# Gate products one unit earlier per section, halves of the experts without barriers, and a paired left one-hot in a two-block transformer kernel

## What is computed

```python
def peer(h, w_query, sub_keys, expert_u, expert_v):
    ...
    gates = jax.nn.softmax(best_v, axis=-1).astype(h.dtype)
    ...
        u = jnp.take(expert_u, xc["idx"], axis=0)
        vv = jnp.take(expert_v, xc["idx"], axis=0)
        a = jax.nn.gelu(jnp.einsum("td,thkd->thk", xc["h"], u))
        return jnp.einsum("thk,thkd->td", xc["g"] * a, vv)
```

## Time and profile before

| | |
|---|---|
| median of 3 runs | 3040.22 us (3030.36 to 3046.02) |
| the profiled execution | 3042.81 us, its span 3041.2 us |
| granted clock of TensorE, mean | 0.967 |
| PE busy | 2880.7 us (95%) |
| PE weight loads busy | 2668.6 us (88%) |
| DVE busy | 2273.0 us (75%) |
| ACT busy | 1364.5 us (45%) |
| POOL busy | 176.4 us (6%) |

### The profile page before, as it was taken

The page is one execution under the profiler, slowest core; times in us unless marked ns, Lnnn a source line. Parts: engine busy times, 40 slices in busy tenths (PEclk is TensorE's granted clock), DMA queues, the critical chain, the costliest instruction groups (busy, mean ns, idle before and its releaser), DMA issues.

```text
span 3041.2 us, 61140 instructions
## 1 busy us (share of the span) xinstructions
PE 2880.7 (95%) x22296; PEld 2668.6 (88%) x22296; DVE 2273.0 (75%) x3797; ACT 1364.5 (45%) x1986; POOL 176.4 (6%) x189
## 2 busy tenths in 40 slices
PE   6998988989989999999999999999999899999998
PEld 5998976889989989989988878799999899988787
DVE  6777834367777668978889978756579888899766
ACT  3445431234444545544434445545455444344454
POOL 0102002100101000020000000000000200000000
PEclk8999986989999999999999999999999999999999
DMA  8885730038867454544445578654445444455554
GB/s 335 302 289 174 242 104 1 1 134 274 302 218 255 142 184 146 180 153 161 161 150 168 166 234 289 216 173 132 160 147 182 153 159 158 148 166 166 165 193 145
DMA packets 150590, 549.51 MB, mean 181 GB/s; under 512 B 16720, under 2 KB 16976, under 8 KB 150224
## 3 DMA queue, kind: packets, MB, share of 16 engines
q1 hardware_dynamic: 127584, 464.05, 45.4%
q0 software_dynamic: 22176, 80.75, 8.0%
q10 hardware_dynamic: 720, 3.17, 0.3%
HBM read 546.86 MB, written 1.05 MB: 180 GB/s over the span
## 4 chain that ended last, share of the span: by engine, by line
PE 69%; DVE 8%; ACT 2%; issue 1%; POOLq 0%; DMA 0%; DVEq 0%; POOL 0%; ACTq 0%
PE acc L2073 15%; PE st L1600 12%; PE st L1604 11%; PE st L1601 11%; PE acc L2079 7%; DVE w_lo L808 3%; PE st L2044 3%; PE acc L1604 1%; PE acc L1601 1%; PE acc L1600 1%; DVE arena L1271 1%; ACT w_hi L424 1%; PE acc L2004 1%; PE st L1651 1%; DVE arena L1306 1%
## 5 line engine op out<-in xcount | busy, mean ns | idle before, releaser
L808 DVE TENSOR_TENSOR w_lo<-ring,w_hi 128x1024 fp32r<-128x1024 f32 x864 | 1076.1, 1247 | 502.2 <-ACT w_hi L424 494.8
L424 ACT ACTIVATE w_hi<-ring 128x1024 fp32r<-128x1024 f32 x864 | 910.5, 1054 | 892.0 <-PE st L1604 798.0
L1600 PE MATMUL st<-h_hi,w_hi 128*128 128x256 f32 x4080 | 1016.3, 287 | 7.0 <-ACT arena L736 3.5
L1601 PE MATMUL st<-h_lo,w_hi 128*128 128x256 f32 x4080 | 1003.7, 284 | 0.0
L1600 PEld LDWEIGHTS st<-h_hi,w_hi 128*128 128x128 f32 x4080 | 783.7, 192 | 20.0 <-issue 11.2
L1601 PEld LDWEIGHTS st<-h_lo,w_hi 128*128 128x128 f32 x4080 | 784.7, 192 | 0.0
L1604 PE MATMUL st<-h_hi,w_lo 128*128 128x256 f32 x4080 | 577.8, 284 | 21.9 <-DVE w_lo L808 21.8
L1604 PEld LDWEIGHTS st<-h_hi,w_lo 128*128 128x128 f32 x4080 | 527.8, 192 | 27.9 <-DVE w_lo L808 27.7
L2073 PE MATMUL acc<-w_hi,act_hi 128*128 128x512 f32 x1016 | 322.6, 399 | 3.9 <-DVE act_lo L1391 3.9
L2073 PE MATMUL acc<-w_hi,act_lo 128*128 128x512 f32 x1016 | 316.1, 392 | 0.0
L769 ACT ACTIVATE act_hi<-arena 128x256 fp32r (+1 forms) x256 | 106.6, 418 | 409.4 <-PE acc L2079 401.1
(11 more groups left out here) (311 smaller groups left out, 2890.2 us busy)
## 6 DMA issues: line engine op xcount, KB each, us to landing
ring<-weights SPq DMA_DIRECT2D x864, 512.0 KB, 3.4
arena<-ada_weights POOLq DMA_DIRECT2D x104, 512.0 KB, 5.0
extra<-ada_weights POOLq DMA_DIRECT2D x48, 512.0 KB, 4.5
arena<-ada_weights SPq DMA_DIRECT2D x16, 512.0 KB, 13.2
arena<-const ACTq DMA_DIRECT2D x1, 2112.0 KB, 10.9
x_t<-params SPq DMA_DIRECT2D x1, 1024.0 KB, 11.3
extra<-crows POOLq DMA_DIRECT2D x2, 512.0 KB, 5.3
out<-arena SPq DMA_DIRECT2D x4, 256.0 KB, 2.2
```

Of the source, the lines that this page charges most:

```text
L424: nc_a.activation(w_hi[:, u % 2, :], ring[:, u % RING, :], ACT.Copy).then_inc(hi_ready, 1)
L808: v.tensor_tensor(w_lo[:, u % 2, :], ring[:, u % RING, :], w_hi[:, u % 2, :], ALU.subtract)\
L1600: mm(dst(t), w, hi_t(t), start=start, stop=False, skip_group_check=True)
L1601: mm(dst(t), w, lo_t(t), start=False, stop=False, skip_group_check=True)
```

## The change

The turns of a half are cut into four sections of eight turns (`SECTIONS`, `PER`). In the last turn of each section there is one unit where there were two (`alone=True`), so from one section to the next the gates come one unit sooner: those of turn 31 now come behind unit 61 and not behind unit 63. The stages `peer_b` and `peer_c` are gone on all engines. In their place ACT waits for the count of multiplies (`g_mult`) ahead of the first `upper` of each half of the rows, DVE waits for all gelus (`gelu`) once, POOL waits for the count of gate products (`g_psum`), and v unit 0 starts the accumulation itself in place of `clear_acc`. `hot_l` is laid out with two tokens innermost, compared with `pair_iota`, so that the weights of one token are read with a step of two.

```diff
+SECTIONS = 4
+PER = TURNS // SECTIONS
...
-        hot_l = [ar(512 * b, 512, base=extra).bitcast(BF16).rearrange("p (t n) -> p t n", t=GROUP) for b in range(2)]
+        hot_l = [hots(512 * b, 512) for b in range(2)]
...
-                def u_half(first, between=None):
+                def u_half(first, between=None, behind=None):
...
                         gelu_of(n)
+                        if n == first + HALF - SECTIONS + 1 and behind is not None:
+                            behind()
                         if n + 1 < first + HALF:
                             step(base + n + 1)
...
-                stage(eng, ST[f"peer_b{l}"])
...
+                def first_gated():
+                    eng.wait_ge(sem("g_mult"), 2 * TURNS * l + TURNS)
+                    upper(0)
+                    upper(1)
+
+                u_half(HALF, behind=first_gated)
...
-                        if n + 2 < first + HALF:
+                        if n + 2 < NKEYS:
                             eng.wait_ge(used, nth(v_base + n))
+                            if n + 2 == HALF:
+                                eng.wait_ge(sem("g_mult"), 2 * TURNS * (l + 1))
                             upper(n + 2)
...
-                    v.tensor_tensor(hot_l[g % 2], keys_t[:, 0, tokens(g, i)].unsqueeze(2).to_broadcast([P, GROUP, NKEYS]),
-                                    kc("iota").unsqueeze(1).to_broadcast([P, GROUP, NKEYS]), ALU.is_equal)\
+                    v.tensor_tensor(hot_l[g % 2], spread(keys_t[:, 0, :], g, i, NKEYS),
+                                    pair_iota.unsqueeze(1).to_broadcast([P, GROUP // 2, NKEYS, 2]), ALU.is_equal)\
...
+                    for part_ in range(SECTIONS):
+                        g, n = PER * part_, (2 * PER - 1) * part_
+                        if part_ == 0:
+                            turn(half, 0, 0)
+                            if half == 1:
+                                eng.wait_ge(sem("gelu"), NKEYS * (l + 1))
+                            g, n = 1, 2
+                        with eng.Fori(0, PER // 2 - 1) as i:
+                            for k in range(2):
+                                turn(half, g + k, n + 2 * k, i)
+                        if part_ > 0:
+                            turn(half, g + PER - 2, n + 2 * PER - 4)
+                        turn(half, PER * part_ + PER - 1, (2 * PER - 1) * part_ + 2 * PER - 2, alone=True)
...
-                stage(eng, ST[f"peer_b{l}"])
+                step(base + NKEYS - 4)
+                step(base + NKEYS - 3)
+                multiply(0, TURNS - 1)
                 lower(0)
                 lower(1)
+                step(base + NKEYS - 2)
+                step(base + NKEYS - 1)
                 turns(1, v_turn)
-                stage(eng, ST[f"peer_c{l}"])
                 v_base = base + NKEYS
-                lower(HALF)
-                lower(HALF + 1)
+                for n in range(HALF - 4, HALF):
+                    if n == HALF - 2:
+                        multiply(1, TURNS - 1)
+                    lower(n + 2)
+                    step(v_base + n)
...
-                for half in range(2):
-                    stage(eng, ST[("peer_b", "peer_c")[half] + str(l)])
                 if l == 0:
+                    eng.wait_ge(sem("g_psum"), 2 * TURNS)
                     eng.dma_start(c_row, crows[1]).then_inc(sem("c_back"), 16)
...
-                                     hot_l[g % 2][:, k, :], hot_r[g % 2][part_][:, k // 2, :, k % 2],
+                                     hot_l[g % 2][:, k // 2, :, k % 2], hot_r[g % 2][part_][:, k // 2, :, k % 2],
...
+                    unit(2)
+                    for part_ in range(SECTIONS):
+                        g, n = PER * part_, (2 * PER - 1) * part_ + 3
+                        with eng.Fori(0, PER // 2 - 1) as i:
+                            for k in range(2):
+                                token_gates(half, g + k, i)
+                                unit(n + 2 * k, i)
+                                unit(n + 2 * k + 1, i)
+                        token_gates(half, g + PER - 2)
+                        unit(n + 2 * PER - 4)
+                        unit(n + 2 * PER - 3)
+                        token_gates(half, g + PER - 1)
+                        unit(n + 2 * PER - 2)
                     unit(HALF - 1)
-                    token_gates(half, TURNS - 1)
...
-                                   w_hi[:, u % 2, 512 * half:512 * half + 512], start=False, stop=False,
+                                   w_hi[:, u % 2, 512 * half:512 * half + 512],
+                                   start=n == 0 and i is None and act_part is act_hi, stop=False,
                                    skip_group_check=True)
...
-                stage(eng, ST[f"peer_b{l}"])
-                clear_acc()
                 turns(1, v_unit)
-                stage(eng, ST[f"peer_c{l}"])
```

More of the change, by code:

```diff
@@ L354, in build @@
         for l in range(LAYERS):
-            for name in ("out", "peer_b", "peer_c", "peer_d"):
+            for name in ("out", "peer_d"):
                 ST[f"{name}{l}"] = len(ST) + 1
@@ L760, in _ @@
                 nc_a.activation(gate_t, st[:, 3, 0:T], ACT.Copy).then_inc(sem("selt"), 1)
-                u_half(HALF)
-                stage(eng, ST[f"peer_b{l}"])
                 def upper(n, i=None):
@@ L769, in upper @@
                     nc_a.activation(act_hi[:, n % 2, :], src, ACT.Copy).then_inc(sem("gated_hi"), 1)
+                def first_gated():
[3 more added lines that the diff above has]
+                u_half(HALF, behind=first_gated)
                 def v_half(first):
                     v_base = base + NKEYS
-                    upper(first)
-                    upper(first + 1)
                     with eng.Fori(0, HALF // 4 - 1) as i:
@@ L1393, in turns, with u_turn @@
                 def turns(half, turn):
-                    turn(half, 0)
-                    with eng.Fori(0, TURNS // 2 - 1) as i:
-                        for g in range(2):
-                            turn(half, 1 + g, i)
-                    turn(half, TURNS - 1)
-                    multiply(half, TURNS - 1)
-                def u_turn(half, g, i=None):
-                    u = base + HALF + 2 * g
+                    for part_ in range(SECTIONS):
[11 more added lines that the diff above has]
+                        turn(half, PER * part_ + PER - 1, (2 * PER - 1) * part_ + 2 * PER - 2, alone=True)
+                def u_turn(half, g, n, i=None, alone=False):
+                    u = base + HALF + n
                     right(half, g, i)
@@ L1409, in u_turn, with v_turn @@
                     left(half, g, i)
-                    step(u + 1, i, 4)
-                def v_turn(half, g, i=None):
-                    u = base + NKEYS + 2 * g
-                    if g < TURNS - 1:
-                        lower(2 * g + 2, i)
+                    if not alone:
+                        step(u + 1, i, 4)
+                def v_turn(half, g, n, i=None, alone=False):
+                    u = base + NKEYS + n
+                    lower(n + 2, i)
                     right(half, g, i)
@@ L1420, in v_turn @@
                         multiply(half, g - 1, i)
-                    if g < TURNS - 1:
-                        lower(2 * g + 3, i)
+                    if not alone:
+                        lower(n + 3, i)
                     left(half, g, i)
-                    step(u + 1, i, 4)
+                    if not alone:
+                        step(u + 1, i, 4)
                 eng.wait_ge(sem("selt"), l + 1)
@@ L2054, in turns @@
                     unit(1)
-                    with eng.Fori(0, TURNS // 2 - 1) as i:
-                        for g in range(2):
-                            unit(2 + 2 * g, i)
-                            token_gates(half, g, i)
-                            unit(3 + 2 * g, i)
-                    unit(HALF - 2)
-                    token_gates(half, TURNS - 2)
+                    unit(2)
[11 more added lines that the diff above has]
+                        unit(n + 2 * PER - 2)
                     unit(HALF - 1)
-                    token_gates(half, TURNS - 1)
                 def v_unit(n, i=None):
```

## The result

The kernel before ran at 3042.05 us (median of 6 runs, 3030.36 to 3046.02), the changed one beside it at 3016.81 us (6 runs, 3009.36 to 3022.20): ratio 0.9923, 95% interval 0.9909 to 0.9937. That is 0.8% faster. The forecast was 3016.5.

A forecast was written before the change was run, and what follows sets the result against it. PE was taken as the bound inside turns (95% busy), DVE close behind. Savings of 22.65 + 1.1 = 23.7 us took the profiled 3042.8 to 3019.1, or 3016.5 for the median, 0.8% less; range 3005 to 3034.

The forecast's parts named there:

- Seams: At the four stages, between u and v units and behind v unit 63 in both layers: 22.65 us lost, to be saved.
- What takes their place at seam b: From u to v units, counted from turn 31's gates: the copy ends near 5.1, 1.4 in hand, so PE never waits.
- Seam c: Ahead of v unit 64: `lower` done at 4.7 to 5 us against 6.28 due, so no wait.
- The shorter left: The compare `left` falls from 1.22 to 0.68 us; directly it saves 1.1 us, at turn 0 of both layers.
- Boundaries: Three per half with one unit less: beside v units 0.35 us in hand, no wait; with the old `left` 0.7 late.
- third rival: `left` stays at 1.22: six boundaries beside v units wait 0.7 each, turn 0 gains nothing; 3022 us, chance 0.06.
- Stepped weights: Gate loads of `hot_l` with a step of two: no change taken, loads staying at 32 ns each at most.
- Loop entries: Loops entered four times per half instead of once: taken as nothing, bounded by -1 and +3 us over the kernel.
- The sum: Whole kernel: 22.65 + 1.1 = 23.7 us off the profiled 3042.8, giving 3019.1, and 3016.5 for the median.
- The second rival: At the four stages' places, part of the waits stays; if half of the loss remains, 3028 us; chance 0.12.

The follow-up runs named there:

- late gates: Changed kernel with the old order of gates and units, no sections, both stages still out and the short `left` kept: 3039.46 us, ratio 0.9997.
- the two kernels with one edit each: Changed kernel with the old turn order but no stages, 3039.46 us; changed kernel with early gates but `peer_b` and `peer_c` put back, 3036.82 us.
- 22 fillers: Changed kernel with 22 useless matmuls in PE's stops at the norms and 14 at the second FFN's: 3018.01 us, beside 3018.42 for the unaltered change.
- both stages back: Changed kernel with sections, early gates and short `left`, but `peer_b` and `peer_c` put back on all engines: 3036.82 us, ratio 0.9986.

## Why the prediction was right, step by step

- **Seams.** Forecast 22.65. Between the first gates and a unit behind the last seam 21.3 are gone, and the turns in between took 60 x 2 x 0.012, or 1.4, longer: 22.7. The seam of layer 0 shown above still loses 0.04. Subtracting steady work between two marks priced the seam without saying what it consists of, and that protected the number: my later estimate by parts, the one in the expectation of the late gates, was too small because it took 1.5 us a seam for the clock where 2.0 and 2.9 were lost.
- **What takes their place at seam b.** Forecast from the last gates: `multiply` at 2.4, `upper` through near 4.0, `lower` near 4.5. The trace: 2.49, 3.93 and 4.42. The copy behind them ends at 5.02 against near 5.1, 1.55 before v unit 0 begins, where 1.4 was forecast. Seam c has no wait.
- **The shorter left.** 0.686 against 0.68. What it pays directly was put at 1.1 us, and the first gates' waits fell by 0.53 each. As the only edit it is not to be seen.
- **Boundaries.** 3.57 to 3.58 beside v units and 3.69 to 3.70 beside u units, without a wait. With the old `left` each boundary beside v units waited 0.68, where 0.7 was forecast: the third rival's mechanism, there to be seen once its condition was made (3022 forecast, 3023.71 measured).
- **Stepped weights.** Taken at nothing, 1.5 us in truth. Loop entries cost nothing visible.
- **The sum.** 23.7 forecast, 20.7 in the profiled executions. The difference is some 1.5 for the weights and 1.8 in stretches that nothing touched. Against 3042.8 the profiled execution gave 3022.2, where 3019.1 was forecast; that the median came within 0.3 us is partly luck, as the medians move by 2 to 4 us from one set of runs to the next (before 3038.1 to 3042.1, after 3016.8 and 3018.4).

The second rival, seams that keep their waits, is what the two kernels with one edit each are. It did not come about because both edits were made.

One reading of rows 3 is a little off: DVE's `lo` starts at 1655.72, 0.06 behind the end of `right` at 1655.66, so not each of DVE's instructions starts before the one ahead has ended. Nothing in the sum hangs on it.

## What to carry to other kernels

Price a seam between two marks in the steady state on both sides, not by the length of the wait in it: behind each stop of 2 to 3.5 us in the two kernels with one edit, matmuls at half the clock lost another 1.6 to 3 us, which the busy times do not show and the granted clock of the windows does. When a barrier goes, ask what chain stands behind it, and move the work as well; here either alone bought nothing or 3 us. The half clock costs its full price only where PE is the bound: at the norms, where DVE fed the rows, full clock bought 0.6 to 1.4 us each in the trace and nothing that could be measured in the time.

## What the runs showed of the hardware

- Matmuls without use, placed in a stop, made a kernel 8.4 us faster (3039.46 to 3031.05; 8.3 by the seams of the traces), with the granted clock at 1.00 instead of 0.52 behind the stop.
- With a rest of 0.74 us of waiting behind 22 fillers (a norm of layer 1) the clock stayed at 1.00; behind a wait of 2.09 (late gates) it was 0.52, where a wait of 0.98 and 24 short gate products stood before. A single stop of 2.52 (both stages back) was also followed by a granted clock of 0.50, from 1570.0 to 1572.9.
- Weights of bf16 that stand 4, 8 and 16 bytes apart take 0.5, 3.7 and 31 ns more per load than packed ones, as the pitch of the turns tells. The durations of the loads (97, 116, 171 ns) overlap each other and show the order, not the price.
- A compare of 1024 elements, all in bf16 with pairs innermost, takes 0.69 us, against 1.22 with an f32 constant and the 128 numbers innermost. No kernel here changes only one of the two, so which of them counts stays open.
